# The last expert's weights in pieces, and another order of the first sums behind the experts

## The reference, cut to what matters

```python
for e in range(N_EXPERTS):
    h = jax.nn.silu(x @ w_gate[e].astype(x.dtype)) * (x @ w_up[e].astype(x.dtype))
    y = y + cw[:, e:e + 1] * (h @ w_down[e].astype(x.dtype)).astype(f32)
...
h = h + hier_moe(rmsnorm(h, g_ffn), ...)
gate = jax.nn.sigmoid(rmsnorm(h, g_ple) @ w_ple_gate.astype(h.dtype))
h = h + (p.astype(h.dtype) @ w_ple_proj.astype(h.dtype)) * gate
...
y_prompt = rmsnorm(hp, g_final)
```

## Time and profile before

| what | us |
|---|---|
| median of three runs (829.55 to 832.31) | 830.74 |
| the profiled execution's own time | 831.13 |
| its span, first to last instruction | 829.3 |
| TensorE busy | 727.8 |
| VectorE busy | 283.5 |
| ScalarE busy | 180.7 |

### The profile page before, as it was taken

The page is one execution under the profiler, slowest core; times in us unless marked ns, Lnnn a source line. Parts: engine busy times, 40 slices in busy tenths (PEclk is TensorE's granted clock), DMA queues, the critical chain, the costliest instruction groups (busy, mean ns, idle before and its releaser), DMA issues.

```text
span 829.3 us, 11240 instructions
## 1 busy us (share of the span) xinstructions
PE 727.8 (88%) x4496; PEld 449.1 (54%) x4496; DVE 283.5 (34%) x504; ACT 180.7 (22%) x278; POOL 102.8 (12%) x161
## 2 busy tenths in 40 slices
PE   8999999999999789899999887777777777778996
PEld 8988899999998534333333322222222222226775
DVE  5556579766434521111101001001001001005875
ACT  7242321323322100111111110000000000004576
POOL 0500000000001112121121111111111111100000
PEclk9999999999999899999999999999999999999999
DMA  9641126572945799999999999999999999995301
GB/s 347 234 180 52 61 80 228 203 261 77 394 155 192 229 393 417 424 427 424 426 427 422 428 425 427 425 427 428 425 428 427 426 427 426 426 422 208 131 27 77
DMA packets 36457, 258.39 MB, mean 312 GB/s; under 512 B 7905, under 2 KB 8465, under 8 KB 22841
## 3 DMA queue, kind: packets, MB, share of 16 engines
q1 hardware_dynamic: 27248, 237.17, 70.0%
q0 software_dynamic: 7072, 19.07, 6.1%
q10 hardware_dynamic: 2096, 1.56, 0.6%
HBM read 251.04 MB, written 15.14 MB: 321 GB/s over the span
## 4 chain that ended last, share of the span: by engine, by line
PE 50%; DMA 35%; DVE 5%; ACT 2%; issue 2%; SPq 0%; DVEq 0%; POOLq 0%; ACTq 0%
DMA arena<-in_w_exp 33%; PE ps L1563 20%; PE ps L1759 15%; PE ps L1776 5%; PE ps L1890 2%; PE ps L1606 1%; PE ps L1678 1%; DMA region_u<-h_rows,index 1%; PE ps L1667 1%; DVE xh L1426 1%; DVE region_u L1379 1%; PE ps L1571 1%; DMA region_m<-y_rows 1%; PE ps L1767 1%; DMA y_rows<-region_v,both_cols 1%
## 5 line engine op out<-in xcount | busy, mean ns | idle before, releaser
L1759 PE MATMUL ps<-arena,region_u 128*64 128x512 f32 x960 | 218.9, 602 | 47.0 <-DMA arena<-in_w_exp 46.0
L1759 PEld LDWEIGHTS ps<-arena,region_u 128*64 128x64 f32 x960 | 67.0, 138 | 196.8 <-issue 124.7
L1375 DVE SCALAR_TENSOR_TENSOR region_u<-ps,small,region_u 128x256 f32<-128x256 f32 x32 | 15.5, 483 | 377.2 <-ACT region_u L864 377.2
L1563 PE MATMUL ps<-u_hi,w_hi 128*128 128x260 f32 x448 | 128.3, 286 | 4.5 <-issue 2.3
L1563 PE MATMUL ps<-u_lo,w_hi 128*128 128x260 f32 x448 | 126.6, 283 | 0.0
L1563 PE MATMUL ps<-u_hi,w_low 128*128 128x260 f32 x448 | 126.5, 282 | 0.0
L1776 PE MATMUL ps<-arena,region_u 128*64 128x512 f32 x480 | 109.6, 598 | 5.9 <-DVE region_u L1379 2.5
L1563 PEld LDWEIGHTS ps<-u_hi,w_hi 128*128 128x128 f32 x448 | 84.3, 188 | 6.2 <-issue 4.2
L1563 PEld LDWEIGHTS ps<-u_hi,w_low 128*128 128x128 f32 x448 | 84.5, 189 | 0.0
L1563 PEld LDWEIGHTS ps<-u_lo,w_hi 128*128 128x128 f32 x448 | 84.4, 188 | 0.0
L685 POOL DMA_INDIRECT y_rows<-region_v,both_cols x32 | 33.4, 1042 | 368.1 <-ACT region_v L868 368.1
(11 more groups left out here) (284 smaller groups left out, 855.8 us busy)
## 6 DMA issues: line engine op xcount, KB each, us to landing
arena<-in_w_exp SPq DMA_DIRECT2D x88, 2048.0 KB, 26.9
arena<-in_w_in SPq DMA_DIRECT2D x35, 512.0 KB, 4.3
region_q<-in_w_exp SPq DMA_DIRECT2D x24, 256.0 KB, 10.3
arena<-in_w_exp SPq DMA_DIRECT2D x8, 512.0 KB, 4.1
arena<-in_w_ple_gate SPq DMA_DIRECT2D x2, 2048.0 KB, 23.5
region_u<-in_xt SPq DMA_DIRECT2D x2, 1040.0 KB, 6.1
arena<-in_state_ret POOLq DMA_DIRECT2D x2, 1024.0 KB, 8.9
xh<-v_few POOLq DMA_DIRECT2D x1, 2048.0 KB, 9.1
```

The lines of the kernel that those rows point to most:

```text
L1375: V.scalar_tensor_tensor(hs[b], ps[:, 2 + b, 256:512], rs[b], sg[b], ALU.mult, ALU.mult).then_inc(out_sem, 1)
L1563: last = mm(halves(out)[:, half, :], w[:, k, :], u[:, cols], start=(k == 0 and s == 0), stop=(k == KD - 1 and s == 2))
L1759: last = mm(ps[side * 64:side * 64 + 64, 2 + b, :], xv[:, k // 4, k % 4, :], rows(k % 4 * 2 + side), start=(k == 0), stop=(k == KD - 1))
```

## The change

The last expert's second gate unit and its down unit are loaded as four transfers of 512 KB each, with a semaphore of their own for each piece (`last_loaded`); the last turn of SP's loop is written out for that. In the last expert `gate_up` waits for one piece in front of each of the steps 4 to 7, and `down` for one piece in front of each `q`; the single wait for the whole down unit is gone there. The waits and the order of use are those of before elsewhere.

In the tail, VectorE's order becomes `gate_low_part(0)`, `combine(1, ...)`, `combine(0, ...)`, `gained(0)`, `gained(1)`, `gate_low_part(1)`, `low_rows(1)`, `gate_low_part(2)`: the first full tile is summed ahead of the sample rows, and the second quarter of the low part goes behind the two `gained`. TensorE transposes turn 1 ahead of turn 0. The sum of turn 0 has a semaphore of its own (`hy_few`), and everyone who waited for `hy_done` waits through `hy_wait`.

```diff
--- before.py
+++ after.py
@@ -97,7 +97,7 @@
 
 
 TAIL_TILES = [NT - 1] + list(range(NT - 1))
-TAIL = [("u", 0), ("u", 1), ("pg", 0)]
+TAIL = [("u", 1), ("u", 0), ("pg", 0)]
 for _n in range(1, NT):
     TAIL += [("pa", _n)] + ([("u", _n + 1)] if _n + 1 < NT else []) + [("pb", _n)]
 TAIL.append(("pc", NT - 1))
@@ -408,6 +408,7 @@
         xg_cleared = sem("xg_cleared")
         xg_loaded = [sem(f"xg_loaded{i}") for i in range(2)]
         out_stored = [sem(f"out_stored{i}") for i in range(2)]
+        last_loaded = [[sem(f"last_loaded{j}{n}") for n in range(PIECES)] for j in range(2)]
         gu_half = sem("gu_half")
         xt_done, xgT_ready, gu_done, silu_done = sem("xt_done"), sem("xgT_ready"), sem("gu_done"), sem("silu_done")
         hs_done, ht_done, hT_ready, down_done, out_ready = (
@@ -416,6 +417,7 @@
         ov = {n: sem("over_" + n) for n in ("w", "xg", "xt", "xgT", "gu", "silu", "hs", "ht", "hT", "down", "out",
                                             "stored")}
         y_loaded = [sem(f"y_loaded{i}") for i in range(2)]
+        hy_few = sem("hy_few")
         hy_done, hy_root, hy_rstd = sem("hy_done"), sem("hy_root"), sem("hy_rstd")
         gate_hi_ready, gate_lo_ready = sem("gate_hi_ready"), sem("gate_lo_ready")
         u3_ready, u3_hi_ready = sem("u3_ready"), sem("u3_hi_ready")
@@ -436,6 +438,10 @@
                 return slot, 16 * turn + (16 * (PIECES - 1) if slot in PIECE_SLOTS else 0)
 
             return slot, i * 16 + (16 * (PIECES - 1) if slot in PIECE_SLOTS else 0)
+
+        def hy_wait(eng, n):
+
+            eng.wait_ge(*((hy_done, n) if n else (hy_few, 1)))
 
         w_pp = region_z[:, 0:2 * D]
 
@@ -561,11 +567,19 @@
             for j in range(6):
                 sp.wait_ge(used[j % 3], 4 + j // 3)
                 load_unit(18 + j, PAIR_SLOTS[j])
-            with sp.Fori(4, NE // 2) as i:
+            with sp.Fori(4, NE // 2 - 1) as i:
                 for j in range(6):
 
                     sp.wait_ge(used[j % 3], i * 2 + (j // 3 - 1))
                     load_unit(i * 6 + j, PAIR_SLOTS[j])
+            for j in range(6):
+                unit, slot = NE * 3 - 6 + j, PAIR_SLOTS[j]
+                sp.wait_ge(used[j % 3], NE - 2 + (j // 3 - 1))
+                if j < 4:
+                    load_unit(unit, slot)
+                for n in range(PIECES if j >= 4 else 0):
+                    at = slice(n * PIECE, n * PIECE + PIECE)
+                    sp.dma_start(ring[:, slot, at], a["w_exp"][unit][:, at]).then_inc(last_loaded[j - 4][n], 16)
             for n, slot in enumerate(GATE_SLOTS):
 
                 sp.wait_ge(gu_done, NE - 1)
@@ -595,7 +609,7 @@
             for n, t in enumerate(TAIL_TILES):
                 r0, m = TILES[t]
                 if n >= 2:
-                    sp.wait_ge(hy_done, n - 1)
+                    hy_wait(sp, n - 2)
                 sp.dma_start(y_buf[n % 2][0:m, :], y_tok[r0:r0 + m, :]).then_inc(y_loaded[n % 2], 16)
             for n, t in enumerate(TAIL_TILES[:-1]):
                 r0, m = TILES[t]
@@ -934,7 +948,7 @@
 
                 t = TAIL_TILES[n]
                 m = TILES[t][1]
-                act.wait_ge(hy_done, n + 1)
+                hy_wait(act, n)
                 link(nc.scalar.activation(gate[n % 2][0:m, :], xh[0:m, t, :], ACT.Square,
                                           accum_out=stats[0:m, 25 + t:26 + t]))
 
@@ -1425,7 +1439,7 @@
                     dve.wait_ge(y_loaded[n % 2], 16 * (n // 2 + 1))
                 ins = V.scalar_tensor_tensor(h, yb[0:m, k * D:(k + 1) * D], wk[0:m, t, k:k + 1], h, ALU.mult, ALU.add)
                 if k:
-                    ins.then_inc(hy_done, 1)
+                    ins.then_inc(hy_done if n else hy_few, 1)
                 else:
                     link(ins)
 
@@ -1461,7 +1475,7 @@
                 g, x, h = gate[n % 2][0:m, :], pp[0:m, t, :], xh[0:m, t, :]
                 at = columns_of(kind, n)
                 dve.wait_ge(act_tail, GATES.index((kind, n)) + 1)
-                dve.wait_ge(hy_done, n + 1)
+                hy_wait(dve, n)
                 link(V.tensor_tensor(x[:, at], x[:, at], g[:, at], ALU.mult))
                 V.tensor_tensor(h[:, at], h[:, at], x[:, at], ALU.add).then_inc(f_done, 1)
 
@@ -1494,13 +1508,13 @@
 
             dve.wait_ge(down_done, NE - 1)
             gate_low_part(0)
-            gate_low_part(1)
+            combine(1, 0)
+            combine(1, 1)
             combine(0, 0)
             combine(0, 1)
-            combine(1, 0)
-            combine(1, 1)
             gained(0)
             gained(1)
+            gate_low_part(1)
             low_rows(1)
             gate_low_part(2)
             gate_rstd(0)
@@ -1753,7 +1767,9 @@
                 xv = xgT[b].rearrange("p (k h r) -> p h k r", h=2, r=ROWS)
                 for k in range(KD):
                     rows, filled, count = units[k // 4]
-                    if k % 4 == 0:
+                    if isinstance(filled, list):
+                        pe.wait_ge(filled[k % 4], 16)
+                    elif k % 4 == 0:
                         pe.wait_ge(filled, count)
                     for side in range(2):
                         last = mm(ps[side * 64:side * 64 + 64, 2 + b, :], xv[:, k // 4, k % 4, :],
@@ -1767,10 +1783,12 @@
                     last = tr(ps[:, 4 + b, k * P:(k + 1) * P], hs[b][:, k * P:(k + 1) * P], ident[:, :])
                 last.then_inc(out_sem, 1)
 
-            def down(b, rows, out_sem):
+            def down(b, rows, out_sem, pieces=()):
 
                 for q in range(4):
                     side_in, k = divmod(q, 2)
+                    if pieces:
+                        pe.wait_ge(pieces[q], 16)
                     hv = hT[b][:, k * P + side_in * 64:k * P + side_in * 64 + 64]
                     for side in range(2):
                         last = mm(ps[side * 64:side * 64 + 64, 6 + b, :], hv, rows(q * 2 + side),
@@ -1790,6 +1808,8 @@
                             units.append((in_spare(j), spare_loaded[j], 16 * i * len(spare[j])))
                         else:
                             units.append((in_ring(slot), slot_filled[slot], filled))
+                    if last and b:
+                        units[1:] = [(in_ring(PAIR_SLOTS[4 + j]), last_loaded[j], 16) for j in range(2)]
                     gate_up(b, units, gu_done, gu_half)
                     parts = parts_of(i, b)
                     for n in parts:
@@ -1803,11 +1823,12 @@
                         rows_t(1 - b, (xg_loaded[1 - b], i * 16 + 16 * (1 + b)), xt_done)
                     pe.wait_ge(hT_ready, e + 1)
                     rows, filled, count = units[2]
-                    pe.wait_ge(filled, count)
+                    if not (last and b):
+                        pe.wait_ge(filled, count)
                     if not first:
 
                         pe.wait_ge(out_ready, e - 1)
-                    down(b, rows, down_done)
+                    down(b, rows, down_done, filled if last and b else ())
 
 
             pe.wait_ge(act_jobs, HEAD.count("A", len(JOBS)))
@@ -1859,7 +1880,7 @@
                     else:
                         pe.wait_ge(act_tail, GATES.index(prev) + 1)
                 if kind == "u":
-                    pe.wait_ge(hy_done, turn + 1)
+                    hy_wait(pe, turn)
                     for k in range(KD):
                         last = tr(b[:, k * P:k * P + m], xh[0:m, t, k * P:(k + 1) * P], ident[0:m, 0:m])
                 else:
```

## The result

| | kernel before | kernel changed |
|---|---|---|
| median of seven runs, us | 830.2 (828.78 to 832.31) | 833.7 (833.01 to 835.05) |
| profiled execution, its span | 831.13, 829.3 | 833.43, 831.6 |

The changed kernel takes 1.005 times as long, with a 95% interval of 1.0035 to 1.0065. That is 3.5 us slower; forecast were 2.4, or 833.1, in a range that holds 833.7. It lies beyond the 0.3% that the forecast drew as its border between "no change" and "slower": slower had been given 0.43, no change the larger chance, 0.52.

What follows compares the result with a forecast made beforehand. Experts run at the pace of weight loads; the end follows the landing of turn 1's rows and the time to `gained(2)`. Pieces 0 plus order +2.4 on the median 830.74 gave 833.1 us, range 831.0 to 834.8.

Steps and rivals of the forecast that it cites:

- The pieces' gain: Last expert's gate units: removing a 1.14 us wait issues the last scatter 1.14 earlier, but its landing does not move.
- The pieces' cost: Weight queue: smaller transfers move 400 GB/s against 426, up to 0.65 us later for everything behind; taken as 0.
- the last rival: Loads in pieces: each small transfer pays a fixed 2.25 us; six more without overlap make 13.5, 846 us; chance 0.02.
- The order: VectorE's tail: work moved behind the landing of turn 1's rows costs 2.4 us, bounds 2.2 to 2.9.
- The clock: TensorE's tail: lower clock after idle 3.1 us makes `pg` wholly slow at 6.4, +3.7 us; rival's chance 0.18.
- The sum: Whole kernel: pieces 0 plus order +2.4 us gives 833.1, own range 832.3 to 833.9; chance 0.52.
- the scatter's length: Sign in the tail: the last scatter, issued about 1.1 us early, takes about 5.4 instead of 4.3.
- VectorE's idle time: Sign in the tail: VectorE stands idle for some 5 us before turn 1's sum.
- `pa` and `gained(2)`: Sign in the tail: `pa` starts near 775.6 and `gained(2)` near 782.4 in the changed profile.
- The scatter didn't gain: Rival at the last scatter: the whole 1.14 us arrives, +1.3 in all, 832.0 us; chance 0.16.
- its engines were not free: Rival at the last scatter: it finds its DMA engines free, rows land 3.2 us earlier, -0.8, 829.9 us; chance 0.07.

Runs made afterwards that it cites:

- held gate: Changed kernel with the second half of `w_ple_gate` issued behind the rows of turns 0 and 1, ScalarE's quarters 2 and 3 behind `high_rows(1)`: 833.01 us, ratio 1.0045.
- Halves: Kernel before with two 1 MB transfers per unit for the last expert's second gate and down units, tail orders as before: 830.78 us, ratio 1.0012 to before.
- long spin: Changed kernel with `SPIN_TAIL` at 64 in place of 48 idle matmuls ahead of the tail: 833.96 us, ratio 1.0051 to the kernel before.
- pieces only: Kernel before with the change's four transfers per unit, VectorE's order and `TAIL` as before: 832.11 us against 828.96, ratio 1.0031.
- order only: Kernel before with whole units, `TAIL` and VectorE's order as in the change: 833.25 us against 828.96, ratio 1.0053.

## Why the forecast was right, and where its terms were off

**The pieces' gain is swallowed: right.** The copy is 1.4 earlier (forecast 1.14), and the scatter loses what that gains, and more. In all seven profiles with eight pieces or four, but for the held gate, it lands 20.4 to 20.6 behind t0; in all four with whole units 20.0 to 20.1. The held gate shows why, and so does the end of the last weights, 0.8 ahead of the landing in every other profile: the scatter has its last rows on the engines that finish the weights last.

The Trainium skill's page "DMA: Bandwidth & Descriptors", section "Queues, rings and completion order", has a DMA engine go round-robin between queue rows, and drain a whole packet of descriptors from one row before it switches. The prediction took from it that most of the earlier issue would arrive. It didn't (6.2 for the scatter with weights queued, 2.36 with half of them held back), and the trace of the changed kernel shows coarse turns: while other engines already moved the scatter, two chains of weights, five rows of 16 KB each, ran without a gap from 752.89 to 755.95, by their spacing on the two engines that end last. That fits with whole packets; how large they are no run here shows.

**The pieces' cost: mis-sized.** The prediction took 0 and held 0.65 as a bound. What came is close to that bound: 4.2 MB at 407 GB/s take 10.3, at 426 they take 9.85, 0.46 more; the last weights end 0.48 later, and the scatter lands 0.5 later. Halves cost 0.35. It was priced from the right row and then set aside for a guess of zero. The Trainium skill's page "DMA: Bandwidth & Descriptors", section "Rules for kernel authors", asks for 1 MiB or more per transfer; here the direction agrees, at half a microsecond, not at the fixed time per transfer that the last rival feared. The fit of 2.0 us that the prediction sets beside that rule is the page's for transfers issued by GpSimd; these are issued by SP.

**The order: right, the exact figure in part by luck.** 2.4 forecast, 2.4 in the kernel that has the order alone, 18.0 from rows to `gained(2)`. The step that the sum of the parts rested on, work moved from under a transfer to behind it, less the waits that it fills, holds. But the forecast's 18.0 was VectorE's own path; by the long spin that path takes 17.5, half a microsecond less, and in the order alone a wait for TensorE, 0.37, fills most of the difference.

**The clock: mis-sized.** The sum had `pg` at 4.8 and nothing for a lower clock beyond 0.2 in one transpose; the rest was a rival: idle 3.1 instead of 1.4, `pg` wholly slow at 6.4, +3.7, deciding once `pg` passes 5.1. The idle stretch was 3.99 and 3.93, `pg` 6.35 and 5.28, both beyond 5.1, and the waits for TensorE 1.57 and 0.48. So the rival came true in part or in whole, on top of the sum. It comes from both parts of the change together: the pieces start the spin 1.4 earlier and land the rows 0.6 later, the order puts the full tile first. With the order alone the stretch is 2.15 and the wait 0.37; in the profile with the spin made longer there is no wait. How much of `pg` is slow is not set by the stretch alone: it differs between executions (6.35 and 5.28 behind nearly the same one, 4.44 behind the 2.53 of pieces only, 3.64 and 5.16 with the longer spin). The Trainium skill's page "TensorE: Matmul & The Clock Gate", section "HAM oscillation — how this bites in real kernels", warns of gaps in which TensorE waits for a DMA; the 0.50 behind the 3.99 agrees. The kernel before has 0.50 behind a wait of 1.42 as well.

Together, from the tables: rows 0.6 later, the order on VectorE 17.5 - 15.6 = 1.9, clock 0.9 to 2.0: 3.4 to 4.5 in the two profiles of the change; the medians say 3.5 and 3.7. The forecast had 0 + 2.4. The 833.7 still lies inside the sum's own range, 832.3 to 833.9, but that range had next to no clock in it: there the two profiles' 0.9 to 2.0 were met by luck. Of the signs to look for, the scatter's length (6.2, said 5.4), VectorE's idle time (6.3, said 5) and `pa` and `gained(2)` (1.0 to 2.2 later behind t0 than said, over the two profiles) erred the same way.

**Against the rivals.** The scatter didn't gain; its engines were not free; small transfers don't pay the 2.25 each that the last rival priced.

**What stays open.** In the first series of runs pieces only, order only and long spin have medians 1.8 to 2.4 further from before's than their tails say (3.2 against 1.0, 4.3 against 2.5, 5.0 against 2.6). The runs of pieces only fall into two groups, 829.5 to 829.7 and 832.0 to 832.4, and the profiled one is of the lower. Something ahead of the last expert differs there; it isn't SP's written-out loop turn (1.0005), and in the later series medians and tails agree within 0.7. The twelve profiles show where such differences arise. The first expert's `down` starts anywhere from 293.4 to 297.3; each of the others keeps its distance to the kernel before to within 0.02 through the twelfth expert, shifts once by up to 1.0 before the thirteenth, and then keeps the new distance to within some 0.3 up to the last expert but one. Of the first series, pieces only and order only, each profiled in one of its faster runs, stand at 294.6 and 294.5; long spin and held gate, profiled in slower ones, at 296.2 and 296.0. Up to there all kernels do the same work, as what the edits change comes later (SP's loop over the loads only ends a turn sooner), so this isn't the mechanism argued above. What makes the stretch longer, and more often in the first series' changed versions than in its kernel before, no experiment here settles. By its median the order alone would be all of the change (1.0053 and 1.0050), by the tails it is 2.5 of 3.4 to 4.5; I go by the tails, whose parts can be seen.

## What to carry to other kernels

Work that fills the wait for a transfer is free only ahead of it: before moving it behind the landing, price it against the time that the moved-up work can save, and count the landing of a transfer over all engines from the engine that is the last to finish other queued data. Issuing a transfer earlier doesn't land it earlier while some engines still have a backlog; what helps there is less queued ahead of it. And where two edits each leave TensorE idle a little longer, price the clock for both stretches together.

## What the hardware showed unexpectedly

SP's part of the issuing, in the changed kernel (start, us, what, count; the time from the first start to the last end):

```profile
715.04 13.79 SPq L582 DMA_DIRECT2D arena<-in_w_exp  x8
730.43 5.44 SPq L586 DMA_DIRECT2D arena<-in_w_ple_gate  x2
```

With eight pieces in the queue the two halves of the gate weights took 5.44 to issue, against 0.81 before and 0.80 with four pieces of 1 MB. In the held gate, which issues one half there behind the same eight pieces, that one took 0.33; so it is the second that is held up. That the length of the queue is the reason is likely, but not tested. Nothing waited for it here. And eight idle matmuls behind the transposes went with `pg` at 3.64, where without them it took 5.2, in one profile each.
